# Decoder trunk with expert rows: an exponential moved four rows up, and two rows in sixteen weighed by VectorE

## The reference, cut to what matters

```python
def peer(h, w_q, k1, k2, u_tab, v_tab):        # per block of 128 positions
    q = (xb @ w_q).reshape(128, 8, 256)        # 8 heads, two halves of 128
    s1 = q[..., :128] @ k1.T; s2 = q[..., 128:] @ k2.T
    v1, i1 = top_k(s1, 16); v2, i2 = top_k(s2, 16)
    top_s, eid = top_k(all sums v1 + v2, 16)   # 16 of 128*128 experts
    gate = softmax(top_s)
    act = gelu(einsum('thkd,td->thk', u_tab[eid], xb))
    return einsum('thk,thkd->td', gate * act, v_tab[eid])
...
x = x + mixer(rmsnorm(x)); x = x + peer(rmsnorm(x), ...)   # twice, then a last rmsnorm
```

## Time and profile before

| | |
|---|---|
| median of 3 runs | 1595.74 us (1595.33 to 1597.86) |
| the profiled execution | 1597.02 us, its span 1595.2 us |
| PE, DVE, ACT, POOL busy | 86%, 65%, 42%, 37% of the span |
| mean granted TensorE clock | 0.952 of full speed |
| gathered by POOL's queue | 545.01 MB of 627.97 MB |

### The profile page before, as it was taken

How to read it: one execution, slowest core, us unless ns; L and a number is a source line. 1 busy time by engine, 2 the same in 40 slices (tenths; PEclk the granted TensorE clock), 3 DMA queues, 4 the chain that set the end, 5 groups by cost and what they waited for, 6 DMA issues and landing times. The chain is left out here.

```text
span 1595.2 us, 15344 instructions
## 1 busy us (share of the span) xinstructions
PE 1374.0 (86%) x4384; PEld 742.3 (47%) x4384; DVE 1039.1 (65%) x2628; ACT 662.1 (42%) x1731; POOL 597.9 (37%) x536
## 2 busy tenths in 40 slices
PE   7999899977777799897978899898988888888776
PEld 6877755533333364443434565344444344443332
DVE  4684566666666666767666656786766566666664
ACT  4653333433333445734343354553443433333333
POOL 0100244444444443433444334233454344345441
PEclk9999999999999899999999999899999999999999
DMA  6876699999999999999999999999999999999997
GB/s 243 303 243 236 266 422 408 393 423 416 422 420 419 410 405 422 422 423 403 423 421 422 421 422 423 405 424 422 398 413 416 422 414 422 422 406 423 419 411 297
DMA packets 98483, 627.97 MB, mean 394 GB/s; under 512 B 11040, under 2 KB 11168, under 8 KB 32352
## 3 DMA queue, kind: packets, MB, share of 16 engines
q0 software_dynamic: 75504, 545.01, 82.9%
q1 hardware_dynamic: 22896, 82.00, 13.6%
HBM read 625.91 MB, written 1.05 MB: 393 GB/s over the span
## 5 line engine op out<-in xcount | busy, mean ns | idle before, releaser
L1128 PE MATMUL psum<-row,diag 128*128 128x512 f32 x2048 | 968.9, 620 | 201.0 <-ACT diag L625 200.7
L437 POOL DMA_INDIRECT row<-in_uv,ids x512 | 585.6, 1144 | 897.9 <-PE psum L1128 702.5
L982 DVE SCALAR_TENSOR_TENSOR row<-row,hn 128x1024 f32<-128x1024 f32 x512 | 616.8, 1224 | 381.9 <-DMA row<-in_uv,ids 371.9
L1128 PEld LDWEIGHTS psum<-row,diag 128*128 128x128 f32 x2048 | 389.9, 198 | 696.2 <-issue 410.1
L607 ACT ACTIVATE acted<-dots 128x2 f32<-128x2 f32 (+1 forms) x257 | 52.2, 203 | 679.9 <-DVE row L982 679.3
L625 ACT ACTIVATE diag<-gate_diag,acted 128x128 f32<-128x128 f32 x512 | 178.0, 387 | 0.2
L616 ACT ACTIVATE gate_diag<-consts,gate 128x128 f32<-128x128 f32 x512 | 173.9, 386 | 0.2 <-DVE gate L974 0.2
L761 DVE TENSOR_TENSOR tile_lo<-raw,tile_hi 128x1024 fp32r<-128x1024 f32 x48 | 58.7, 1224 | 54.6 <-ACT tile_hi L470 54.6
L470 ACT ACTIVATE tile_hi<-raw 128x1024 fp32r<-128x1024 f32 x48 | 50.7, 1058 | 72.6 <-PE psum L1128 68.7
L1128 PE MATMUL psum<-raw,hT_mix 128*128 128x512 f32 x152 | 71.4, 592 | 0.0
L1128 PEld LDWEIGHTS psum<-hT_query,raw 128*128 128x128 f32 x480 | 58.8, 194 | 14.3 <-issue 14.3
(11 more groups left out here) (194 smaller groups left out, 1054.6 us busy)
## 6 DMA issues: line engine op xcount, KB each, us to landing
raw<-in_a_in SPq DMA_DIRECT2D x32, 512.0 KB
raw<-in_w_q SPq DMA_DIRECT2D x32, 512.0 KB
raw<-in_b_rv SPq DMA_DIRECT2D x32, 512.0 KB
raw<-in_a_out SPq DMA_DIRECT2D x16, 512.0 KB
raw<-in_b_qk SPq DMA_DIRECT2D x16, 512.0 KB
row<-in_uv,ids POOLq DMA_INDIRECT x512
early_q<-in_w_q SPq DMA_DIRECT2D x12, 512.0 KB, 4.5
raw<-in_b_out SPq DMA_DIRECT2D x6, 512.0 KB
```

Source lines behind the costliest of these rows:

```text
L437: pool.indirect_dma_start(rows[s][:, :], None, t[f"uv{l}"][:, :], bass.IndirectOffsetOnAxis(ids[:, h, g, k:k + 1], 0)).then_inc(row_loaded ...
L982: dve.scalar_tensor_tensor(u, u, 1.0, hn[:, h, :], ALU.mult, ALU.mult, accum_out=dots[:, h, g, k:k + 1]).then_inc(dotted, 1)
L1128: return pe.matmul(o, a, b, start=start, stop=stop, skip_group_check=True)
```

## The change

Three things are done. `exp(j)` on ACT moves from behind row k = 11 to behind row k = 7. Rows with k = 3 and k = 11 (64 of 512) are no longer multiplied by PE; DVE adds them to `x` itself (`add_row`), two rows later: behind the dots of k = 5 and k = 13. ACT no longer spreads or weighs for these rows, the ring of diagonals counts only the 448 others, and POOL waits for `row_added` instead of `row_used` where the slot held such a row.

```diff
+ADDED = (3, 11)
+ADD_LAG = 2
...
+def is_added(n):
+    return n % TOPK in ADDED
+def added_rows(n):
+    return len(ADDED) * (n // TOPK) + sum(k < n % TOPK for k in ADDED)
+def product_rows(n):
+    return n - added_rows(n)
...
-                if n >= ROW_SLOTS:
-                    pool.wait_ge(row_used, n - ROW_SLOTS + 1)
+                old = n - ROW_SLOTS
+                if old >= 0 and is_added(old):
+                    pool.wait_ge(row_added, added_rows(old + 1))
+                elif old >= 0:
+                    pool.wait_ge(row_used, product_rows(old + 1))
...
                 for c in range(BATCH):
-                    if n + BATCH + c < 2 * ROWS:
+                    if n + BATCH + c < 2 * ROWS and not is_added(n + BATCH + c):
                         spread_gate(n + BATCH + c)
...
-                    weigh(n + c)
+                    if not is_added(n + c):
+                        weigh(n + c)
...
                 j = done // TOPK + 1
-                if done % TOPK == TOPK - 4 and j < GROUPS:
+                if done % TOPK == TOPK // 2 and j < GROUPS:
                     exp(j)
...
+            def add_row(n):
+
+                _, h, g, k = group_of(n)
+                m = added_rows(n)
+                dve.wait_ge(gelu_done, n // BATCH + 1)
+                dve.wait_ge(gates_ready, n // TOPK + 1)
+                if m >= 2:
+                    dve.wait_ge(row_added, m - 1)
+                dve.tensor_tensor(add_weight[:, m % 2:m % 2 + 1], gate[:, h, g, k:k + 1], acted[:, h, g, k:k + 1], ALU.mult).then_inc(added_weight, 1)
+                dve.wait_ge(added_weight, m + 1)
+                if m >= 1:
+                    dve.wait_ge(row_added, m)
+                dve.scalar_tensor_tensor(x[:, h, :], rows[n % ROW_SLOTS][:, D:2 * D], add_weight[:, m % 2:m % 2 + 1], x[:, h, :],
+                                         ALU.mult, ALU.add).then_inc(row_added, 1)
...
+                if is_added(n - ADD_LAG):
+                    add_row(n - ADD_LAG)
                 if k == TOPK // 2 - 1 and j < GROUPS and j not in (2 * P_HEADS, 3 * P_HEADS):
                     choose(j)
...
-                pe.wait_ge(diag_ready, n + 1)
...
+                if not is_added(n):
+                    m = product_rows(n)
+                    pe.wait_ge(diag_ready, m + 1)
```

More of the change, by code:

```diff
@@ L277, in trunk @@
         head_inv = sb("head_inv", [P, TT])
+        add_weight = sb("add_weight", [P, 2])
         psum = ctx.enter_context(nc.psum_tensor("psum", [P, 8, BANK], F32))
@@ L317, in trunk @@
         dotted, gelu_done, diag_ready, row_used = sem("dotted"), sem("gelu_done"), sem("diag_ready"), sem("row_used")
+        row_added, added_weight = sem("row_added"), sem("added_weight")
         glr_done, glr_copied, la_done, z_ready, la_abs, la_exp, la_ln, la_ready = (
@@ L612, in spread_gate @@
                 _, h, g, k = group_of(n)
+                m = product_rows(n)
                 act.wait_ge(gates_ready, n // TOPK + 1)
-                if n >= 2 * BATCH:
-                    act.wait_ge(diag_ready, n - 2 * BATCH + 1)
-                act.activation(gate_diag[:, n % (2 * BATCH), :], ident, ACT.Copy, scale=gate[:, h, g, k:k + 1]).then_inc(gate_spread, 1)
+                if m >= 2 * BATCH:
+                    act.wait_ge(diag_ready, m - 2 * BATCH + 1)
+                act.activation(gate_diag[:, m % (2 * BATCH), :], ident, ACT.Copy, scale=gate[:, h, g, k:k + 1]).then_inc(gate_spread, 1)
             def weigh(n):
                 _, h, g, k = group_of(n)
-                act.wait_ge(gate_spread, n + 1)
+                m = product_rows(n)
+                act.wait_ge(gate_spread, m + 1)
                 act.wait_ge(gelu_done, gelus[0])
-                if n >= DIAGS:
-                    act.wait_ge(row_used, n - DIAGS + 1)
-                act.activation(diag[:, n % DIAGS, :], gate_diag[:, n % (2 * BATCH), :], ACT.Copy, scale=acted[:, h, g, k:k + 1]).then_inc(diag_ready, 1)
+                if m >= DIAGS:
+                    act.wait_ge(row_used, m - DIAGS + 1)
+                act.activation(diag[:, m % DIAGS, :], gate_diag[:, m % (2 * BATCH), :], ACT.Copy, scale=acted[:, h, g, k:k + 1]).then_inc(diag_ready, 1)
             def mix(h, w):
@@ L1032, in mix @@
                 if w == SUMS:
-                    add_sums(2, h, base, [(row_used, PICKS * (h + 1))] * 2)
+                    dve.wait_ge(row_added, added_rows(PICKS * (h + 1)))
+                    add_sums(2, h, base, [(row_used, product_rows(PICKS * (h + 1)))] * 2)
                 if w == ROOT:
@@ L1108, in _ @@
                     if w == SUMS:
-                        add_sums(4, 0, 4, [(row_used, 3 * PICKS)] * 2)
+                        dve.wait_ge(row_added, added_rows(3 * PICKS))
+                        add_sums(4, 0, 4, [(row_used, product_rows(3 * PICKS))] * 2)
                     if w == ROOT:
@@ L1117, in _ @@
                     gates(j)
-            add_sums(4, 1, 6, [(last_row_half, 1), (row_used, 2 * ROWS)])
+            dve.wait_ge(row_added, added_rows(2 * ROWS))
+            add_sums(4, 1, 6, [(last_row_half, 1), (row_used, product_rows(2 * ROWS))])
             add_eps(4, 1)
@@ L1435, in _ @@
                 w = n % PICKS
-                pe.wait_ge(diag_ready, n + 1)
[L1437 to L1444, removed]
+                if not is_added(n):
+                    m = product_rows(n)
+                    pe.wait_ge(diag_ready, m + 1)
+                    if l == 1 and w == 0:
+                        pe.wait_ge(x_ready[3], 2 * h + 2)
+                    for d in range(2):
+                        ins = product(psum[:, 4 + 2 * h + d, :], diag[:, m % DIAGS, :], rows[n % ROW_SLOTS][:, D + d * BANK:D + (d + 1) * BANK],
+                                      start=w == 0, stop=w == PICKS - 1)
+                        if n == 2 * ROWS - 1 and d == 0:
+                            ins.then_inc(last_row_half, 1)
+                    ins.then_inc(row_used, 1)
                 c = FIRST_Q + n // QUERY_ROWS
```

## The result

The changed kernel takes 1598.97 us (median of 20 runs, 1596.58 to 1601.05), the kernel before in the same rounds 1595.8 us (20 runs). The ratio is 1.0017, its 95% interval 1.0011 to 1.0023. The forecast was 1590.6 us, in a range up to 1597.0. The profiled execution took 1601.05 us with a span of 1599.0 us. It is the slowest of the 20, 2.1 us above their median; that of the kernel before was 1.2 us above its own.

A forecast was written before the change was run, and what follows sets the result against it. The prediction took the DMA engines at their ceiling (422 GB/s) as the bound. Its terms, -5.0 - 3.6 + 0.5 + 3.0 = -5.1 us, took the profiled 1597.0 to 1591.9, a median of 1590.6 us; range 1585.5 to 1597.0.

The forecast's parts named there:

- exponential: At four dips behind VectorE's waits at `gates`: 8.0 us lost, moving it returns 3.6 to 7.6, taken as -5.0.
- TensorE without rows: Windows 255 to 270 and 285 to 316 us: relieved PE keeps pace with DMA; -3.6 us, bounds 0 and 3.9.
- VectorE with adds: Mixer groups, where idle cover is partly gone: adds push the choice; +0.5 us, bounds 0 to +5.
- the end: Last four rows, behind the idle gap row 507 leaves: PE at half clock; +3.0 us, bounds 0 and +3.6.
- rival A: All dip windows: dips are DMA's own, not want of gathers, only the tail counts; say 1596.5 us; chance 0.24.
- Rival C: Dots of k = 6 and 7: adds push the choice; 1622.6 us, in mixer groups alone 1606; chance 0.06.
- Rival D: POOL's next gather: an add holds its issue, 1.28 us in six windows, +7.7, 1598.3 us; chance 0.03.

The follow-up runs named there:

- first48_exp_back: Changed kernel with adds only among rows 0 to 47 (six rows) and the exponential back behind k = 11; 1593.39 us, ratio 0.9987.
- adds_first48: Changed kernel with rows added only among rows 0 to 47 (six instead of 64), the exponential moved; 1593.14 us, ratio 0.9985.
- exp_alone: Kernel before with the exponential moved alone, all 512 rows still on PE; 1596.44 us, ratio 0.9999.
- adds_not_last: Changed kernel without adds in the last group (rows 499 and 507 back on PE); 1595.91 us, ratio 1.0005.
- first48_light_both: adds_first48 with TensorE's products (a stretch's first and last row excepted) and VectorE's dots cut in rows 48 to 495, sums incomplete; 1593.50 us.
- adds_alone: Changed kernel with the exponential back behind k = 11, all 64 adds kept; 1598.07 us, ratio 1.0012.
- first48_idle_adds: adds_first48 plus weight-zero adds on VectorE behind k = 5 and 13 of rows 48 to 495, freeing no slot; 1595.16 us.
- first48_light_dve: adds_first48 with VectorE's dot over only 512 of 1024 numbers in rows 48 to 495; 1593.78 us, ratio 0.9988.
- first48_choice_filled: adds_first48 with 84 matmuls of zeros on TensorE behind each row k = 7 in groups without mixer work; 1594.27 us.

## Why the prediction was wrong

It came out 8.4 us too low. By its own terms, with medians:

| term | forecast | measured | from |
|---|---|---|---|
| exponential | -5.0 | -0.3 | first48_exp_back to adds_first48; in exp_alone a ratio of 0.9999 |
| TensorE without rows | -3.6 | -2.4 | before (1595.8) to first48_exp_back |
| VectorE with adds | +0.5 | +2.8 | adds_first48 to adds_not_last |
| the end | +3.0 | +3.1 | adds_not_last to the changed kernel |
| sum | -5.1 | +3.2 | |

**The step that failed** is the one on the exponential: "While it sits there no dot is made, no slot comes free, and gathers dry up some rows later", and the 8.0 us counted from it. Its first clause is true, the second is not, and the third did not matter. Slots came free at TensorE's own pace during the wait. More than that, I took length x (1 - rate/422) of a short window for time that could be got back. Light_both closes 7.4 us of these dips, and its rows 64 to 495 take 1193.2 us, as before. This was rival A for rows 48 on, with the reason that I had written for it (the share of the DMA engines stays at 0.94 or more while the rate falls). I held against it that each dip had a wait ahead of it; that the one stands ahead of the other was no cause. Rival A was wrong of the first 48 rows: there the two windows closed and the time fell.

**TensorE without rows** was right in place, and within its bounds in size (-2.4; the two windows alone give -3.8, and the dots 0 to 64 are 3.2 to 4.3 us faster wherever TensorE is relieved): its window went from 412 to 421 GB/s. What was taken from TensorE elsewhere was worth nothing, as forecast. **The end** was right in its cause, and its tail grew by 2.9 us, from 10.5 to 13.4. That the forecast of 10 us for the last four rows reads 10.03 is in part luck: adds_alone has the same gap, and there they took 8.52 us (last section).

**VectorE's adds** were right in duration and mis-sized in cost: +0.5 became +2.8 us for rows 48 to 495. No working stood behind the +0.5; the 0.35 us for each of fourteen groups is that of the upper bound, 4.9. VectorE's own load is what costs (first48_idle_adds). Rival C had the direction; whether the adds cost by pushing choices no run shows, and 1606 us never came near. **Rival D** was put at nothing by a misread row. The gather of 1564.56 began before the dot of 1564.87, so that it could not show what a running dot does to an issue. Gathers that begin while a dot runs are held in the same trace, and those that begin while an add runs are held in the changed kernel's; the last section shows both. By the rule of the Trainium skill, "SBUF — State Buffer", section "Who interferes with whom", a VectorE instruction with two SBUF inputs contends with a GpSimd instruction that reads SBUF; the trace agrees, and my sentence that it doesn't was wrong. The price of rival D still didn't appear: the dots had been holding issues all along, so that the mean of an issue did not grow with 64 adds (1144 ns before, 1141 now), and a shorter issue gained no time (first48_light_dve).

The bounds were added wrongly too. The least of the exponential, nothing from TensorE, 5 for the adds and 3.6 for the end are +5.0 us, and not +3.6.

**What stays open.** In rows 48 to 495 the rate over 1200 us is 418 GB/s with TensorE and VectorE at half load and 417 before, while single windows reach 422 to 424. What makes this difference of 1%, and why a dip closed in one place opens in another, no run here tells. Nor do they tell at which rows VectorE's 72.5 us of idle adds cost 2.0 us when 226 us less of its work gain nothing, nor how long the low clock lasts behind a gap.

## What to carry to other kernels

Before a dip in the transfer rate is counted as a gain, halve the work of the engine that is blamed for it and time that: one kernel with work left out, such as first48_light_both, would have struck the -5.0 us from the sum. Compare the whole stretch, best by the rows that it holds, and not the dip alone. Relieve an engine only where it is over its due (here the six rows below row 48, -2.4 us) and leave it alone in the last group, where an idle gap ahead of the final products costs more than the work that it saves: of 64 moved rows six paid, and no kernel is faster than the one with these alone, 1593.14 us, by what can be measured.

## What the runs showed of the hardware

A gap of 2.98 us ahead of the last products was enough for TensorE's lower clock, which cost 10.03 - 7.13 = 2.9 us; with a gap of 1.42 us, behind 1.73 us of matmuls on zeros, it stayed at full speed. The gap does not fix the price. In adds_alone it is the same, and by windows of 2 us the granted clock was back at 1.00 some 2.8 us into the work (0.50 from 1582 to 1584, a mean of 0.89 from 1584 to 1586). In the changed kernel that took 5.9 us (0.50 up to 1588, 0.76 from 1588 to 1590). The last rows of adds_alone:

```profile
1581.64 8.52 PE L1173 MATMUL psum<-row,diag 128*128 128x512 f32 x16 [2.99 <-ACT diag L649]
```

A low clock off the path costs nothing: in first48_light_both the mean was 0.861, in first48_choice_filled 0.974, and the second is no faster.

A running dot holds a gather's issue on POOL. In time, from the kernel before:

```profile
233.84 1.23 DVE L982 SCALAR_TENSOR_TENSOR row<-row,hn 128x1024 f32<-128x1024 f32 x1 [1.26 <-DMA row<-in_uv,ids]
233.92 1.96 POOL L437 DMA_INDIRECT row<-in_uv,ids  x1 [0.54 <-PE psum L1128]
```

The issue ends 0.81 us after the dot. So do nearly all of the 209 gathers in that trace that were begun while a dot ran: they took 1430 ns on average, the other 303 took 946. The adds do the same: in the changed kernel a gather begun at 264.58, behind an add at 264.42, took 1.94 us.

With less to hold it the issue gets shorter. The mean was 1138 ns in adds_first48; with VectorE's dots halved it fell to 1018 (first48_light_dve), and with TensorE's products halved as well to 1006. Groups by line, of adds_first48 and of first48_light_both:

```profile
L459 POOL DMA_INDIRECT row<-in_uv,ids x512 | 582.8, 1138 | 898.0 <-PE psum L1173 703.6
```

```profile
L459 POOL DMA_INDIRECT row<-in_uv,ids x512 | 515.2, 1006 | 963.9 <-PE psum L1174 701.9
```

That is 132 ns a gather, 68 us in all, and none of it was on the path.
